# A residual added by two accumulating transfers, and two weight blocks loaded four groups ahead

## The reference, cut to what matters

```python
hm = _rms(x, norm_mlp) @ w_up                    # 2048 -> 8192
x = x + jnp.square(jax.nn.relu(hm)) @ w_down     # 8192 -> 2048
...
y_prompt = _rms(xp, norm_final)
```

## Time and profile before

| | us |
|---|---|
| median of 3 runs | 2585.13 (2584.07 to 2585.49) |
| the profiled execution | 2583.3 |
| its span | 2581.5 |
| PE busy | 2544.1 |
| DVE busy | 2010.5 |
| ACT busy | 1162.2 |

### The profile page before, as it was taken

How to read it: one execution, slowest core, us unless ns; L and a number is a source line. 1 busy time by engine, 2 the same in 40 slices (tenths; PEclk the granted TensorE clock), 3 DMA queues, 4 the chain that set the end, 5 groups by cost and what they waited for, 6 DMA issues and landing times.

```text
span 2581.5 us, 46954 instructions
## 1 busy us (share of the span) xinstructions
PE 2544.1 (99%) x19624; PEld 2476.6 (96%) x19624; DVE 2010.5 (78%) x2500; ACT 1162.2 (45%) x1616; POOL 173.8 (7%) x277
## 2 busy tenths in 40 slices
PE   8999999999999999999999999999999999999997
PEld 7889999999999979899999999999999999999997
DVE  8889888763686663478888888888878888888888
ACT  6445444441453341245555556655633333333344
POOL 1000000010000020000111110000010000000000
PEclk9999999999999999999999999999999999999999
DMA  8663333362334385433566665555586565555532
GB/s 301 206 210 123 107 105 110 115 222 87 131 127 158 124 318 207 171 116 108 184 223 222 223 220 202 195 212 192 216 313 246 194 208 191 192 191 208 193 131 102
DMA packets 134435, 471.44 MB, mean 183 GB/s; under 512 B 12480, under 2 KB 18752, under 8 KB 122976
## 3 DMA queue, kind: packets, MB, share of 16 engines
q1 hardware_dynamic: 92176, 259.74, 30.6%
q0 software_dynamic: 41648, 208.62, 21.8%
q10 hardware_dynamic: 416, 0.30, 0.0%
HBM read 381.08 MB, written 87.54 MB: 182 GB/s over the span
## 4 chain that ended last, share of the span: by engine, by line
PE 91%; DVE 5%; DMA 1%; issue 1%; ACT 1%; DVEq 0%; ACTq 0%; SPq 0%
PE psum_main L2856 27%; PE psum_side L2856 20%; PE psum_main L2442 15%; PE psum_main L2570 11%; PE psum_side L2570 8%; PE psum_main L2546 3%; PE psum_main L2499 2%; DMA unit_raw<-weights 1%; PE psum_main L2501 1%; PE psum_main L2780 1%; DVE unit_low L2121 1%; PE psum_main L2708 1%; PE psum_side L2749 1%; PE psum_side L2649 1%; ACT unit_high L1309 1%
## 5 line engine op out<-in xcount | busy, mean ns | idle before, releaser
L1309 ACT ACTIVATE unit_high<-unit_raw 128x1024 fp32r<-128x1024 f32 x384 | 400.7, 1055 | 530.9 <-PE psum_main L2856 154.1
L2121 DVE TENSOR_TENSOR unit_low<-unit_raw,unit_high 128x1024 fp32r<-128x1024 f32 x384 | 468.1, 1223 | 108.7 <-ACT unit_high L1309 108.5
L2856 PE MATMUL psum_main<-tokens_late,unit_high 128*128 128x272 f32 x2048 | 388.5, 288 | 3.4 <-DVE hidden L2223 2.3
L2856 PE MATMUL psum_main<-hidden,unit_high 128*128 128x272 f32 x1984 | 377.2, 288 | 4.1 <-DVE residual_late L2253 2.3
L2856 PEld LDWEIGHTS psum_main<-tokens_late,unit_high 128*128 128x128 f32 x2048 | 321.8, 189 | 4.2 <-DVE hidden L2223 3.0
L2856 PEld LDWEIGHTS psum_main<-hidden,unit_high 128*128 128x128 f32 x1984 | 312.1, 189 | 5.2 <-DVE residual_late L2253 3.3
L2856 PE MATMUL psum_main<-tokens_late,unit_low 128*128 128x272 f32 x1024 | 295.0, 288 | 0.0
L2856 PE MATMUL psum_side<-tokens_late,unit_high 128*128 128x272 f32 x1536 | 293.1, 288 | 1.5 <-issue 0.8
L2570 PE MATMUL psum_main<-tokens,unit_high 128*128 128x272 f32 x1536 | 291.9, 288 | 2.0 <-ACT queries L1159 1.0
L2856 PE MATMUL psum_main<-hidden,unit_low 128*128 128x272 f32 x992 | 286.1, 288 | 0.0
L2856 PE MATMUL psum_side<-hidden,unit_high 128*128 128x272 f32 x1488 | 283.7, 288 | 0.0
(11 more groups left out here) (331 smaller groups left out, 5031.2 us busy)
## 6 DMA issues: line engine op xcount, KB each, us to landing
unit_raw<-weights SPq DMA_DIRECT2D x438, 512.0 KB, 4.3
hidden<-hidden_kept POOLq DMA_DIRECT2D x56, 1088.0 KB, 6.5
hidden_kept<-hidden_staged POOLq DMA_DIRECT2D x31, 1904.0 KB, 7.4
unit_sum<-weights SPq DMA_DIRECT2D x44, 512.0 KB, 3.6
residual<-x_t POOLq DMA_DIRECT2D x16, 544.0 KB, 6.5
residual_kept<-residual_new POOLq DMA_DIRECT2D x32, 272.0 KB, 2.3
cache_ring_q<-cache_k POOLq DMA_DIRECT2D x8, 1024.0 KB, 6.1
cache_low_a<-cache_v POOLq DMA_DIRECT2D x8, 1024.0 KB, 11.0
```

Source lines behind the costliest of these rows:

```text
L1309: act.activation(WHI[:, slot, :], raw, ACT.Copy).then_inc(mlp_high, 1)
L2121: dve.tensor_tensor(WLO[:, slot, :], raw, WHI[:, slot, :].bitcast(F32), ALU.subtract) \
L2856: ins = pe.matmul(bank, w[:, slot, col:col + P], moving[:, k, part, :], start=start and k == 0 and n == 0, stop=k == kk - 1 and n == 2, sk ...
```

## The change

The residual is not loaded at the start of the down half. The first two contributions to each quarter of each tile are not both added to it: the first one is written (`tensor_scalar` with 1 or -1, 16 instructions in groups n = 0 to 3), and everything after is added as before. The residual is added later, by two transfers of 8 tiles each (2176 KB) that accumulate into `residual_late` instead of overwriting it: the first is queued in group n = 6, the second in n = 8. DVE waits for them at the first add of groups n = 8 and n = 10. The stores of the last two groups move up, next to each other.

The top blocks w11 and w12 of group 32 get a place of their own, `unit_early`, in tiles of `residual_late` that nothing uses by then, and SP loads them behind the blocks of group 28 instead of behind those of group 32. The readers of `w11` and `w12` of group 32 take them from there. The first add of group n = 2 waits for all hidden stores, because it now writes tiles that the stores read.

```diff
@@ buffers
+        EARLY = at("unit_early", [P, 2, UNIT], F32, b_at)
@@ SP, for q in range(2 * QUADS)
-                    sp.wait_ge(mlp_sum, 4 * q)
-                    sp.dma_start(into(q, RAW[:, 0, :]), w11).then_inc(block_raw[0], 16)
-                    sp.wait_ge(mlp_ready, PRODUCTS * (q - 1) + 6)
-                    sp.dma_start(into(q, RAW[:, 1, :]), w12).then_inc(block_raw[1], 16)
+                    if q != QUADS:
+                        sp.wait_ge(mlp_sum, 4 * q)
+                        sp.dma_start(into(q, RAW[:, 0, :]), w11).then_inc(block_raw[0], 16)
+                        sp.wait_ge(mlp_ready, PRODUCTS * (q - 1) + 6)
+                        sp.dma_start(into(q, RAW[:, 1, :]), w12).then_inc(block_raw[1], 16)
+                    if q == QUADS - 4:
+                        sp.wait_ge(scale_stored, 16)
+                        for n in range(2):
+                            sp.wait_ge(x_spilled[n], 2 * SPILLED + 16 * KT // 2)
+                        for n, w in enumerate(blocks(QUADS)[0:2]):
+                            sp.dma_start(into(QUADS, EARLY[:, n, :]), w).then_inc(early_loaded, 16)
@@ POOL
-            def bring_back(n, t0, t1):
-                pool.dma_start(X2[:, t0:t1, :], x_kept[t0:t1].rearrange("t p n -> p t n")).then_inc(x_back[n], 16)
+            def add_back(n, t0, t1):
+                pool.wait_ge(down_read, PRODUCTS * (4 + t1 // 4))
+                pool.dma_start(X2[:, t0:t1, :], x_kept[t0:t1].rearrange("t p n -> p t n"), accum_op=ALU.add) \
+                    .then_inc(x_back[n], 16)
...
-                    bring_back(0, 0, 4)
...
-            pool.wait_ge(stage_ready, 2 * QUADS)
-            bring_back(1, 4, 9)
             store_hidden(QUADS - 2)
-            pool.wait_ge(hid_stored, 16 * (QUADS - 1))
-            bring_back(2, 9, KT)
             store_hidden(QUADS - 1)
...
                     load_hidden(c, i)
+                    if c == 2 and i == 4:
+                        add_back(0, 0, CH)
+                    if c == 3 and i == 0:
+                        add_back(1, CH, KT)
@@ DVE, add_down
-                if n < 4:
-                    for piece in ((0,), (1,), (1, 2), (2,))[n]:
-                        dve.wait_ge(x_back[piece], 16)
+                if n == 2 and i == 0:
+                    dve.wait_ge(hid_stored, 16 * QUADS)
+                if n in (8, 10) and i == 0:
+                    dve.wait_ge(x_back[(n - 8) // 2], 16)
...
-                dve.tensor_tensor(out, out, bank, op).then_inc(down_read, 1)
+                if n < 4 and i in (0, 2, 3, 6):
+                    ins = dve.tensor_scalar(out, bank, 1.0 if op == ALU.add else -1.0, None, ALU.mult)
+                else:
+                    ins = dve.tensor_tensor(out, out, bank, op)
+                ins.then_inc(down_read, 1)
```

## The result

The changed kernel takes 2600.14 us (median of 6 runs, 2599.18 to 2603.66), the kernel before 2584.86 beside it (6 runs, 2583.91 to 2588.64): a ratio of 1.006, 95% interval 1.005 to 1.007. It is slower by 0.6%, 15 us, and outside the range that I gave. The profiled execution took 2600.8 us, its span 2599.1.

The account below looks back on a forecast made before the run. PE, busy 99% of the span, bounds the kernel, so only its gaps count. 2583.3 - 3.9 (seam) + 2 x 3.2 (adds) = 2585.8, plus 1.8 from profiled execution to median: 2587.6 us, range 2580.5 to 2598.

Parts of the forecast that it names:

- the seam's five gaps: PE gaps where the halves meet, 5.26 us together: 1.63, 0.39, 0.50 and 1.41 go, 1.33 stays.
- what the seam is worth: Gain where the up and down halves meet: 3.93 us, bounds 2.0 and 5.26.
- the store that moves up: Third rival, at the seam: moved stores meet group 33's blocks, gain only 2.0 us, time 2589.5; chance 0.05.
- the landing of w12: Last weight block issued in group 6, beside an add: lands 10.8 us after issue at plain rate, 13.4 at half.
- the room: Group 6: w12 has 1.7 us of room; an add costs its landing after issue minus 8.9 us.
- The lower edge, 1.9: Groups of the accumulating transfers: cost of 1.9 us per add at plain rate, from w12 landing after 10.8 us.
- Per add: Cost of each accumulating transfer through delayed weights in groups 6 to 7 and 8 to 9: 3.2 us.
- The first rival: Groups of the adds: they hold the engines for the weights' whole time; 2595.6 us, or 2601 slower still; chance 0.32.
- its mark: Sign of the first rival: w12 takes over 13.5 us from issue to landing; two adds then cost 9.1 us.
- its second price: First rival's slower case: 10 us per add, 2601 us.
- Choosing the middle: Add cost taken as 3.2 us, the middle of 1.9 at plain rate and 4.5 at half rate.
- what costs nothing: Early blocks, multiplications (at most 1 us over 84, beside PE), DVE's wait at n = 2, and POOL's queue: no cost.

Follow-up runs that it names:

- without the early blocks: Changed kernel with both adds three products later, and w11 and w12 of group 32 loaded as before the change: 2583.21 us, ratio 0.9991 to the kernel before.
- late adds and the waiting store: Changed kernel with both adds three products later, and group 30's store waiting for group 31's hidden rows as before: 2577.87 us, ratio 0.997 to the kernel before.
- late adds: Changed kernel with both accumulating transfers queued three products later, behind the hidden tile that follows product 3: 2581.12 us, ratio 0.9987 to the kernel before.

## Why the prediction was wrong

- **Right: the seam's five gaps**. Those of 1.63, 0.39, 0.50 and 1.41 went. The reason given is shown for the first alone: without the early blocks it is back. The 0.39 had the same reason and isn't back there; the slow matmuls behind the 2.86 us gap (0.66 over 5 us) may hide it. The 1.33 went too, which I had only as a bound; with late adds and the waiting store 0.83 of it is left.
- **Wrong: what the seam is worth.** I took 3.93 us and gave a chance of 0.05 to the store that moves up. It did meet the blocks of group 33: 2.55 us of gap, some clock with it, and 2.6 us of gain in place of 3.9. With the store held back and the adds late the landmarks give the seam 5.6 us, though gaps of 0.83 and 0.26 us are left in it. PE's idle time there fell by 4.3 us only; the other 1.3 us are busy time (147.0 us against 145.7 for the same 1159 matmuls), and I can't place them.
- **Wrong, the step that failed: the landing of w12.** The prediction had 10.8 us at plain rate and 13.4 at half rate with a row to a packet; measured are 12.6 and 18.9. The packets and their turns were as that line had them. Three terms were not. The packet takes 186 ns and not 166 (1.3 us). The 2.1 us that the queues leave free were subtracted, but nearly nothing of them came to pass. And the hidden tile, 2.7 us, which I put behind w12, was ahead of it. Corrected, the line reads 4.9 + 11.9 + 2.7 = 19.5 against 18.9, and 4.9 + 5.3 + 2.7 = 12.9 against 12.6.
- **Wrong: the room.** I looked at the last block only, and took its 8.9 us from group 1. There PE waited at 1936.66 for an add of DVE, which had fallen behind, and not for w12 itself; its own room is 10.7. By itself this error went the other way, but the 8.9 held, without my seeing it, what DVE's lateness adds behind a late w12: 18.9 - 8.9 = 10.0 us is nearly the 10.3 measured. So the line's form was good and its landing term wrong. What I left out is w21, the second block issued: it has 9.7 us, and beside a plain transfer it sets the time (6.5 us per transfer, where I had 1.9). The lower edge, 1.9, was therefore not to be had at all in that place.
- **Left out: the clock.** I priced a gap at its length. PE was busy for 7.8 us more than before, all of it behind gaps. How much of that is a loss differs: behind each add's first gap none, since w12 was waited for anyway; behind the second no more than what a wait for DVE took where the clock stayed. Beside the plain transfers PE lost 2.0 and 1.6 us above the one gap of each: there the slow matmuls, or a wait that they hid, came on top.
- **Per add** I took 3.2 us out of 1.9 to 7.2. Measured are 10.3. The first rival came true for its stated reason: the adds share the engines for the weights' whole time, and its mark, 13.5 us until w12 lands, was passed by 5. That its second price, 10 us per add and 2601 us, fits so well is luck: it stood there without any working, and it leaned on a seam worth 3.9 us.
- **Choosing the middle.** I had a cited rule for half rate and no row against it, and still took the mean of plain and half rate. With half rate taken as it stood, 4.5 per add, the forecast would have been 2590, still short, but the chance of slower would have been the larger one.
- **Right: what costs nothing.** DVE never waited at n = 8 or 10 (the adds land 22.5 us after issue, of 42), the multiplications leave no gap (DVE busy 2010.7 against 2010.5), and the wait for the last hidden stores leaves none in n = 2.

## What to carry to other kernels

A bulk transfer that nobody needs for 42 us can still cost 10 us: ask which small loads are issued while it runs, and how late each of them may land, every one and not only the last. Put it into the pause between two sets of such loads; here 9 us later made 19 us of difference for two transfers, while cutting them in halves made things worse. And a gap of TensorE can cost more than its length, because the clock may fall behind it; but ask first what PE would have waited for next. Beside the adds w12, and then DVE, would have taken nearly all of that time anyway.

## What the runs showed of the hardware that I had not expected

- An accumulating transfer moves packets of one row (2.2 KB, 186 to 188 ns each), where a plain one of the same shape moves 4.2 KB in 166 ns. Beside weights in turn it lands in 22.5 us, with no weights beside it for most of the way in 19.2; a plain one beside weights takes 13.8.
- Behind a gap of about 2 us the granted clock stayed in some rows and fell in others, at matmuls of the same shape: 1.00 behind 2.11 us without the adds, 2.02 us with plain transfers, 1.89 us with one add and 2.21 us with four; but 0.66 over 5 us behind 2.08 us with late adds and behind 1.76 and 2.11 us in the changed kernel. Behind the gaps from 2.35 to 5.18 us it had fallen each time, to between 0.50 and 0.73 over a window of 5 us behind it. What decides at 2 us is open.
